# A hybrid decoder block on one core: mixer A's scores as three products of split operands, with selected and local keys side by side

## What is computed

```python
p_cmp = softmax(q_raw @ kc)                      # compressed keys, 15 of them
o_cmp = p_cmp @ vc
ks = rope(k_slc)                                 # selected branch: 256 tokens are 4 blocks,
p = softmax(mask(q_rot @ ks)); o_slc = p @ vs    # top 16 of 4 blocks, so all causal keys
num, _, den = band_attention(q_rot, rope(k_win), v_win, 511)   # local branch: window over 256 tokens
o = gates[..., 0:1] * o_cmp + gates[..., 1:2] * o_slc + gates[..., 2:3] * num / den
```

## Time and profile before

| what | value |
|---|---|
| median of 3 executions | 1837.71 us |
| the profiled execution | 1837.62 us, span 1835.8 us |
| granted TensorE clock | full (1.00) over the span |
| TensorE busy | 1824.1 us, 99% |
| VectorE, ScalarE, GpSimd busy | 1062.3, 823.3, 188.8 us |
| DMA | 344.78 MB, 188 GB/s on average |

### The profile page before, as it was taken

One profiled execution on the slowest core, in us unless ns is written; L12 is line 12 of the kernel. 1 busy time (PEld: TensorE's weight loads), 2 busy tenths in 40 slices (PEclk: granted clock), 3 DMA queues, 4 the chain that ended last, 5 costly groups with the idle time before them and its releaser, 6 DMA issues.

```text
span 1835.8 us, 23379 instructions
## 1 busy us (share of the span) xinstructions
PE 1824.1 (99%) x8474; PEld 1512.7 (82%) x8474; DVE 1062.3 (58%) x1097; ACT 823.3 (45%) x1062; POOL 188.8 (10%) x161
## 2 busy tenths in 40 slices
PE   9999999999999999999999999999999999999998
PEld 7888878888888888888888888888888888888886
DVE  7856656556665665644564456445644584445444
ACT  6644454444544435444444444444444464444442
POOL 2220002200202020022002200220022000000000
PEclk9999999999999999999999999999999999999999
DMA  9866677546455464666566656665666667776665
GB/s 290 249 194 186 190 230 222 167 124 189 129 168 164 128 182 127 183 186 193 162 193 186 193 162 192 187 191 163 188 190 190 177 184 218 211 210 204 214 206 193
DMA packets 183928, 344.78 MB, mean 188 GB/s; under 512 B 15136, under 2 KB 19360, under 8 KB 183840
## 3 DMA queue, kind: packets, MB, share of 16 engines
q1 hardware_dynamic: 182992, 342.45, 64.1%
q10 hardware_dynamic: 848, 1.07, 0.2%
HBM read 339.27 MB, written 4.19 MB: 187 GB/s over the span
## 4 chain that ended last, share of the span: by engine, by line
PE 98%; DVE 1%; DMA 0%; ACT 0%; issue 0%; DVEq 0%; ACTq 0%
PE acc L445 30%; PE acc L447 30%; PE acc L446 30%; PE trans L459 2%; PE heads L488 2%; PE scores L473 2%; PE acc L606 1%; PE heads L527 0%; DVE y L1291 0%; PE scores L595 0%; PE scores L506 0%; DMA xt_raw<-in_x_t 0%; PE trans L516 0%; ACT w_parts L717 0%; PE trans L649 0%
## 5 line engine op out<-in xcount | busy, mean ns | idle before, releaser
L947 DVE TENSOR_TENSOR w_parts<-raw,w_parts 128x1024 fp32r<-128x1024 f32 x624 | 779.9, 1251 | 695.6 <-ACT w_parts L717 695.2
L717 ACT ACTIVATE w_parts<-raw 128x1024 fp32r<-128x1024 f32 x624 | 660.3, 1059 | 735.3 <-PE acc L447 728.3
L445 PE MATMUL acc<-w_parts,x_parts 128*128 128x512 f32 x2432 | 961.1, 395 | 3.7 <-DVE w_parts L947 1.7
L447 PE MATMUL acc<-w_parts,x_parts 128*128 128x512 f32 x2432 | 948.2, 390 | 0.0
L446 PE MATMUL acc<-w_parts,x_parts 128*128 128x512 f32 x2432 | 947.0, 389 | 0.0
L447 PEld LDWEIGHTS acc<-w_parts,x_parts 128*128 128x128 f32 x2432 | 456.5, 188 | 97.4
L445 PEld LDWEIGHTS acc<-w_parts,x_parts 128*128 128x128 f32 x2432 | 456.9, 188 | 96.2 <-issue 5.0
L446 PEld LDWEIGHTS acc<-w_parts,x_parts 128*128 128x128 f32 x2432 | 457.1, 188 | 91.3
L400 POOL TENSOR_TENSOR rot<-tok_a,trig 128x512 f32<-128x512 f32 x26 | 41.1, 1579 | 1127.6 <-ACT tok_a L723 936.3
L729 ACT ACTIVATE probs_t<-trans 128x512 f32<-128x512 f32 (+1 forms) x44 | 26.2, 596 | 88.0 <-PE trans L459 81.0
L1199 DVE RECIPROCAL mixed<-mixed 128x256 f32<-128x256 f32 x32 | 55.9, 1747 | 0.5
(11 more groups left out here) (151 smaller groups left out, 581.2 us busy)
## 6 DMA issues: line engine op xcount, KB each, us to landing
raw<-in_w_in SPq DMA_DIRECT2D x480, 512.0 KB, 3.6
raw<-in_w_out SPq DMA_DIRECT2D x128, 512.0 KB, 4.5
raw<-in_w SPq DMA_DIRECT2D x16, 512.0 KB, 4.5
x_tok<-in_x SPq DMA_DIRECT2D x16, 256.0 KB, 4.9
xt_raw<-in_x_t SPq DMA_DIRECT2D x7, 512.0 KB, 5.9
out<-y SPq DMA_DIRECT2D x5, 512.0 KB, 2.9
wpost<-in_post_w SPq DMA_DIRECT2D x8, 256.0 KB, 4.9
gate_raw<-in_w_in SPq DMA_DIRECT2D x1, 768.0 KB, 8.0
```

What stands on the lines that cost most here:

```text
L445: nc.tensor.matmul(o, stat_hi, w_hi[:, s, kk, 0:width], start=(k == 0), stop=False)
L447: last = nc.tensor.matmul(o, stat_lo, w_hi[:, s, kk, 0:width], start=False, stop=(k == KB - 1))
L717: nc.scalar.activation(w_hi[:, n % SPLIT_SLOTS, :, 0:width], raw[:, n % RAW_SLOTS, :, 0:width], ACT.Copy).then_inc(hi_ready, 1)
L947: V.tensor_tensor(w_lo[:, s, :, 0:width], raw[:, n % RAW_SLOTS, :, 0:width], w_hi[:, s, :, 0:width].bitcast(F32), ALU.subtract).then_inc(l ...
```

## The change

Queries and keys of mixer A's selected and local branches are kept as first parts and rests (`q_hi`, `q_lo`, `k_hi`, `k_lo`), and the keys of both branches lie side by side, so that one product takes a head's query against both branches. A unit is now one tile and both branches: 2 heads of tile 0 (2 x 2 x 128 keys) or 1 head of tile 1 (2 x 256 keys); there are again six. Where a unit was 2 or 4 float32 matmuls it is 3 or 6 of F32R operands. The first parts come from ScalarE (`first_parts`, in the place of the old copies), the rests from VectorE (`rest_parts`), behind its split of the step; `tr_free` is counted up by VectorE for these fills. The selected keys are copied as they are and split later in two big operations. The values' products keep their number. Mixer B only has its arguments renamed.

```diff
+PAIRED = [(0, 0, 2), (0, 2, 2), (1, 0, 1), (1, 1, 1), (1, 2, 1), (1, 3, 1)]
...
+        k_hi, _ = sb("k_hi", [P, 2, HPG, SEQ], F32R, offset=late)
+        k_lo, _ = sb("k_lo", [P, 2, HPG, SEQ], F32R, offset=region + 4 * KB // 2 * SEQ)
+        q_hi, _ = sb("q_hi", [P, HPG, SEQ], F32R, offset=r_off)
+        q_lo, _ = sb("q_lo", [P, HPG, SEQ], F32R, offset=region + 4 * KB // 2 * SEQ + 4 * 2 * HPG * SEQ)
+        ksl_t, _ = sb("ksl_t", [P, HPG, SEQ], offset=p_off)
...
+            def paired_scores(u, unit, g, fills):
+
+                t, h0, nh = PAIRED[u]
+                pe.wait_ge(tr_free, fills)
+                pe.wait_ge(scores_free, unit)
+                nk = P * (t + 1)
+                for i in range(nh):
+                    o = scores[:, 2 * nk * i:2 * nk * (i + 1)]
+                    q = [part[:, h0 + i, t * P:(t + 1) * P] for part in (q_hi, q_lo)]
+                    keys = [part[:, :, g, 0:nk] for part in (k_hi, k_lo)]
+                    nc.tensor.matmul(o, q[0], keys[0], start=True, stop=False)
+                    nc.tensor.matmul(o, q[0], keys[1], start=False, stop=False)
+                    last = nc.tensor.matmul(o, q[1], keys[0], start=False, stop=True)
+                last.then_inc(scores_done, 1)
+
+            def paired_values(u, g, fill):
+
+                t, h0, nh = PAIRED[u]
+                pe.wait_ge(tr_free, fill + 1)
+                for i in range(nh):
+                    for branch in range(2):
+                        for b in range(t + 1):
+                            blk = (2 * i + branch) * (t + 1) + b
+                            last = nc.tensor.matmul(heads[:, t, (h0 + i) * P:(h0 + i + 1) * P],
+                                                    probs_t[:, u % 2, blk * P:(blk + 1) * P],
+                                                    v_tok[:, branch, b, bass.ds(P * g, P)],
+                                                    start=False, stop=(branch == 1 and b == t), skip_group_check=True)
+                return last
...
                 if 6 <= n <= 11:
                     u = n - 6
-                    keys = lambda h, nk: k_t[:, u // 3, g, 0:nk]
-                    unit_scores(u % 3, unit + 1 + u, qrot_t, keys, fill + 4)
+                    if u == 0:
+                        pe.wait_ge(ksplit_ready, 1)
+                    paired_scores(u, unit + 1 + u, g, fill + 4)
...
+            def first_parts(fill, dst, ready):
+
+                act.wait_ge(tr_done, fill + 1)
+                nc.scalar.activation(dst, trans[:, :].rearrange("p (h t) -> p h t", h=HPG), ACT.Copy).then_inc(ready, 1)
...
-                    take_fill(FILL_KSL + t, k_t[:, 0, :, t * P:(t + 1) * P])
+                    take_fill(FILL_KSL + t, ksl_t[:, :, t * P:(t + 1) * P])
...
+                if at == 1:
+                    act.wait_ge(weights_used, PAIRS * (C_CMP + 1))
+                    nc.scalar.activation(k_hi[:, 0, :, :], ksl_t[:, :, :], ACT.Copy).then_inc(khi_ready, 1)
...
-                    take_fill(FILL_KW[t], k_t[:, 1, :, t * P:(t + 1) * P])
+                    first_parts(FILL_KW[t], k_hi[:, 1, :, t * P:(t + 1) * P], khi_ready)
...
                     if at in (4, 5):
-                        take_fill(fill + at - 2, qrot_t[:, :, (at - 4) * P:(at - 3) * P])
+                        first_parts(fill + at - 2, q_hi[:, :, (at - 4) * P:(at - 3) * P], qhi_ready)
...
+            def rest_parts(fill, dst, hi, ready, count):
+
+                dve.wait_ge(tr_done, fill + 1)
+                dve.wait_ge(ready, count)
+                V.tensor_tensor(dst, trans[:, :].rearrange("p (h t) -> p h t", h=HPG), hi.bitcast(F32), ALU.subtract
                                 ).then_inc(tr_free, 1)
...
+                if at == 1:
+                    dve.wait_ge(khi_ready, 1)
+                    V.tensor_tensor(k_lo[:, 0, :, :], ksl_t[:, :, :], k_hi[:, 0, :, :].bitcast(F32), ALU.subtract
+                                    ).then_inc(ksplit_ready, 1)
+                if at in (5, 8):
+                    t = (at - 5) // 3
+                    cols = slice(t * P, (t + 1) * P)
+                    rest_parts(FILL_KW[t], k_lo[:, 1, :, cols], k_hi[:, 1, :, cols], khi_ready, 2 + t)
...
                     split(c, n)
+                    if at in (4, 5):
+                        cols = slice((at - 4) * P, (at - 3) * P)
+                        rest_parts(fill + at - 2, q_lo[:, :, cols], q_hi[:, :, cols], qhi_ready, TILES * g + at - 3)
```

More of the change, by code:

```diff
@@ L222, in build @@
         tr_free = sem("tr_free")
+        qhi_ready = sem("qhi_ready")
+        khi_ready = sem("khi_ready")
+        ksplit_ready = sem("ksplit_ready")
         scores_done = sem("scores_done")
@@ L531, in attention_a @@
                     u = n - 10
-                    values = lambda h, b: v_tok[:, u // 3, b, bass.ds(P * g, P)]
-                    last = unit_values(u % 3, u, values, fill + 6 + u, False, u >= 3)
+                    last = paired_values(u, g, fill + 6 + u)
                     if n == PAIRS - 1:
@@ L729, in take_fill, with exp_unit @@
                 nc.scalar.activation(dst, src, ACT.Copy, scale=scale).then_inc(tr_free, 1)
-            def exp_unit(u, slot, unit):
-                t, h0, nh = UNITS[u]
+            def first_parts(fill, dst, ready):
+                act.wait_ge(tr_done, fill + 1)
+                nc.scalar.activation(dst, trans[:, :].rearrange("p (h t) -> p h t", h=HPG), ACT.Copy).then_inc(ready, 1)
+            def exp_unit(t, slot, unit):
                 nk = P * (t + 1)
+                nh = NC // nk
                 act.wait_ge(max_ready, unit + 1)
@@ L839, in attention_a_frame @@
                     if 6 <= at <= 11:
-                        exp_unit((at - 6) % 3, (at - 6) % 4, unit + 1 + at - 6)
+                        exp_unit(PAIRED[at - 6][0], (at - 6) % 4, unit + 1 + at - 6)
             def mixing_frame(c, tiles_mixed):
@@ L872, in _ @@
                         u = (at - 1) // 2
-                        exp_unit(u, u, UNIT_B + u + UNITS_B * g)
+                        exp_unit(UNITS[u][0], u, UNIT_B + u + UNITS_B * g)
             def square(n, parity):
@@ L1117, in _, with mask_unit @@
             evacuate(C_QA0, 0, tok_a[:, 1, :], rq1)
-            def mask_unit(u, slot, unit, bias):
-                t, h0, nh = UNITS[u]
+            def mask_unit(t, slot, unit, bias):
                 nk = P * (t + 1)
+                nh = NC // nk
                 b = (bias[:, 0:P] if t == 0 else bias[:, P:3 * P]).unsqueeze(1).broadcast_to([P, nh, nk])
@@ L1129, in mask_unit, with normalise_unit @@
                 V.tensor_reduce(negmax[:, slot, 0:nh], p, AX.X, ALU.max, negate=True).then_inc(max_ready, 1)
-            def normalise_unit(u, slot, unit, recips, weights=None, gate=None):
-                t, h0, nh = UNITS[u]
+            def normalise_unit(t, slot, unit, recips, weights=None, gate=None):
                 nk = P * (t + 1)
+                nh = NC // nk
                 p = probs[:, slot, :].rearrange("p (h n) -> p h n", h=nh)
@@ L1140, in normalise_unit @@
                 if gate is not None:
-                    V.tensor_tensor(weight[:, slot, 0:nh], f, gate, ALU.mult).then_inc(weight_done, 1)
+                    w = weight[:, slot, 0:nh]
+                    V.tensor_tensor(w.rearrange("p (h b) -> p h b", b=2), f.rearrange("p (h b) -> p h b", b=2), gate,
+                                    ALU.mult).then_inc(weight_done, 1)
                     f = weight[:, slot, 0:nh]
@@ L1144, in normalise_unit, with attention_a_frame @@
                 V.tensor_tensor(p, p, f.unsqueeze(2).broadcast_to([P, nh, nk]), ALU.mult).then_inc(probs_ready, 1)
-            def attention_a_frame(c, g, unit):
+            def attention_a_frame(c, g, unit, fill):
                 for n in range(LEAD, PAIRS + LEAD):
@@ L1165, in attention_a_frame @@
                         u = at - 6
-                        mask_unit(u % 3, u % 4, unit + 1 + u, causal)
+                        mask_unit(PAIRED[u][0], u % 4, unit + 1 + u, causal)
                     split(c, n)
+                    if at in (4, 5):
+                        cols = slice((at - 4) * P, (at - 3) * P)
+                        rest_parts(fill + at - 2, q_lo[:, :, cols], q_hi[:, :, cols], qhi_ready, TILES * g + at - 3)
                     if at == 4:
@@ L1181, in attention_a_frame @@
                         u = at - 7
-                        t, h0, nh = UNITS[u % 3]
-                        normalise_unit(u % 3, u % 4, unit + 1 + u, 6 * g + u, 6 * g + u,
-                                       gates[:, t, bass.ds(HPG * g + h0, nh), 1 + u // 3])
+                        t, h0, nh = PAIRED[u]
+                        normalise_unit(t, u % 4, unit + 1 + u, 6 * g + u, 6 * g + u,
+                                       gates[:, t, bass.ds(HPG * g + h0, nh), 1:3])
             def mix_tile(at, group):
@@ L1233, in _ @@
                         u = (at - 1) // 2
-                        mask_unit(u, u, UNIT_B + u + UNITS_B * g, dilated)
```

(1 more changed line is left out.)

9 lines of the change are left out of this document (5 added, 4 removed).

## The result

The changed kernel takes 1842.38 us (median of 11 runs, 1842.01 to 1843.09) against 1838.1 us for the kernel before (11 runs, 1837.61 to 1840.09): a ratio of 1.0024, with a 95% interval from 1.0016 to 1.0031. It is slower by 4.3 us.

A forecast was written before the change was run, and what follows sets the result against it. The prediction took TensorE, busy 99%, to bound the kernel. Waits of 7.9, 0.9 and 0.4 us less 4.1 for cheaper scores gave +5.1 on 1837.62, so 1842.7 us, with an 8-in-10 range of 1838.4 to 1846.0.

The forecast's parts named there:

- TensorE is the bound: Whole kernel: TensorE is busy 99% of the span, so a wait put into its queue is paid in full.
- The eight waits: Mixer A, steps 5 and 6 of four frames: TensorE waits 0.98 and 1.00 us for banks VectorE frees; 7.9 us.
- The turn of 4.19: Mixer A, step 4 to 5: time in us from transposes through VectorE's rest to TensorE's next transposes, against 3.21 before.
- All six terms: Mixer A's bank chain: to copy 0.63, ScalarE split 0.49, VectorE split 1.09, next operation 1.14, rest 0.69, hand-over 0.15 us.
- The third case: Rival, mixer A's bank chain: shorter than added up, about 0.5 us a wait, 1838.4 us; chance 0.13.
- The gain: Mixer A's scores: units fall from 0.855 us to 0.69 (tile 0) and 0.68 (tile 1); 4.1 us over four frames.
- The case in which 256 columns cost as much as 512: Rival, tile 0's score products: no cheaper at half the width, 5.4 us more, 1848.1 us; chance 0.08.
- The keys' wait at step 9 of C_QA0: Local keys in C_QA0: the rest ends at 327.24, TensorE goes on at 327.39 instead of 326.48; 0.9 us.
- The selected keys' rest: C_QA0, step 1: VectorE's 1024-column rest delays the split and copy of `hidden`, so TensorE waits 0.4 us; bounds 0 to 0.9.
- The rule of the Trainium skill: VectorE's next operation starts only once the pipe is empty: each of nine turns 0.09 us longer, +5.9 instead of +5.1.
- The issue gap of the Trainium skill: Score products on TensorE: 0.109 us for 256 columns and 0.216 for 512, which would make the saving 4.9 us.
- Faster, if the waits do not bind: Rival, mixer A's bank: the rest runs ahead of VectorE's split, only cheaper scores remain, 1833.5 us; chance 0.06.

The follow-up runs named there:

- the hand-over: Kernel before, float32 scores kept, but a VectorE subtraction behind its split frees the rotated queries' bank at steps 4 and 5 of mixer A's frames: 1845.74 us.
- the second subtraction: Changed kernel with one more unused VectorE subtraction ahead of each rest of the rotated queries, eight in all: 1846.94 us.
- the product left out: Changed kernel with rests ahead of VectorE's splits, without the product of queries' first parts and keys' rests: 1828.11 us.
- one branch a product: Changed kernel with rests ahead of VectorE's splits, each score product over one branch's keys, twice as many at half the width: 1839.24 us.
- the selected keys' second subtraction: Changed kernel with one more unused 1024-column VectorE subtraction for the selected keys at step 1 of C_QA0: 1843.83 us.
- the version with the rests first: Changed kernel with VectorE's rests of rotated queries and local keys ahead of its split of the same step, all work kept: 1833.63 us.

## Why the prediction was right, and where not

The forecast was +5.1 us, by the waits; measured are +4.3 between the medians and +4.4 between the spans. Put right term by term, as below, its sum is 8.0 + 0.8 + 0 - 4.3 = +4.5. By its steps:

- **TensorE is the bound.** Right. Edits that put time between TensorE's instructions or took it away were paid nearly one to one: the hand-over 8.07 for 8.0, the second subtraction 4.56 for 4.8, the product left out 5.52 for 5.5. Two came out higher than expected, one branch a product with 5.6 for 5.0 and the selected keys' second subtraction with 1.45 for 0.94; what is known of the difference stands with them.
- **The eight waits, 7.9 us.** Measured 8.0 in steps (0.97 and 1.03 in the first frame) and 8.07 when put in alone. The turn of 4.19 was 4.18 and 4.22. All six terms held, the hand-over of 0.15 and the rest at 0.68 for 0.69 among them. The third case, waits of half the size, falls.
- **The gain, 4.1 us.** Measured 1.08 a frame, 4.3 us; the median of the version with the rests first is 4.0 under the kernel before. A product of 256 columns costs 0.117, taken at 0.115; the difference lies in steps 8 and 9, which were given the mean of the other four units and save 0.44 us together where the sum had 2 x 0.855 - 2 x 0.68 = 0.35. The case in which 256 columns cost as much as 512 falls.
- **The keys' wait at step 9 of C_QA0, 0.9.** It is 0.81 (4.10 against 3.29 us). The chain up to the rest was right; TensorE went on nearer to its end than 0.15 us:

```profile
322.94 0.60 PE L469 MATMUL trans<-cst,rot 128*128 128x128 f32 x4
326.30 0.68 DVE L1011 TENSOR_TENSOR k_lo<-trans,k_hi 128x512 fp32r<-128x512 f32 x1
327.04 1.92 PE L688 MATMUL trans<-w_sb,gelu 128*16 128x128 f32 x16 [0.74 <-DVE k_lo L1011]
```

  The rest ends at 326.98, and TensorE's next instruction starts 0.06 later.
- **The selected keys' rest, 0.4 us.** This is the mis-sized term: it costs nothing. The prediction let the split behind it run at 1.65 us, because the one of the kernel before did, beside GpSimd. In the changed kernel VectorE's queue has no gap there, and it is GpSimd that takes longer. Its subtraction for the rotation of the local keys, in the changed kernel, with VectorE's three operations beside it and TensorE's step 3:

```profile
301.72 5.62 POOL L414 TENSOR_TENSOR rot<-rot,rot_tmp 128x256 f32<-128x256 f32 x1
304.40 1.21 DVE L1163 TENSOR_TENSOR k_lo<-ksl_t,k_hi 128x1024 fp32r<-128x1024 f32 x1
305.53 1.21 DVE L994 TENSOR_TENSOR w_parts<-raw,w_parts 128x1024 fp32r<-128x1024 f32 x1
306.67 0.41 DVE L1147 COPY hidden<-trans 128x256 f32<-128x256 f32 x1
307.43 0.99 PE L667 MATMUL trans<-cst,junk 96*128 96x48 f32 x8
```

  The same operation of GpSimd, in the kernel before:

```profile
301.95 3.35 POOL L404 TENSOR_TENSOR rot<-rot,rot_tmp 128x256 f32<-128x256 f32 x1
```

  It is stretched from 3.35 to 5.62 us and ends 0.60 us after the recorded end of VectorE's last long subtraction, and rest and split both run at 1.21 us. This is the lower end that the prediction had named for this term, 0. The copy of `hidden` ends at 307.08, and TensorE's step 3 comes 3.66 us after step 2, as before. One more such subtraction was needed to see a wait.
- **The rule of the Trainium skill (VectorE: DVE Perf Modes, The DRAIN you can't avoid).** The forecast named an estimate of +5.9 for it. The section adds, as the forecast did not, that an operation which is not held starts earlier. Here too the rest starts 1.14 us after a split of 1.23, and the nine turns have no 0.09 more in them. The measurements stand against taking the rule into such a chain.
- **The issue gap of the Trainium skill (TensorE: Matmul & The Clock Gate, Back-to-back issue gap).** By it the estimate of the gain was 4.9; measured are 4.3. Its 0.109 at 256 columns is 0.117 here, its 0.216 at 512 is 0.227. The section gives these as gaps of an isolated matmul, and 0.131 us at 512 for a stream of weight loads and matmuls; the measured 0.227 is further from that.
- **Faster, if the waits do not bind.** The case had named what it takes, a rest ahead of the split, and 1833.5 us for it. The change does not do that; the kernel that does takes 1833.63.

## What to carry to other kernels

When a buffer with one slot changes the engine that frees it, add up the whole chain from the producer's start to its next turn: every operation that stands ahead of the new last one in its queue, and those ahead of what that one waits for, and compare with the producer's own step. A saving on the bound engine can be real (4.3 us here) and be outweighed twice over by such a turn that is 1 us too long; moving one operation ahead of its neighbour, on either engine, got it back here. In this kernel split operands paid in tile 0 only because the products stayed wide: price the product at its real width before replacing a float32 one.

## What the runs showed of the hardware

- A product of the split type costs 0.227 us at 512 columns, 0.117 at 256 and 0.111 at 128. Halving the width from 256 to 128 brings next to nothing: three products of 128 columns (0.33 us) are dearer than the two instructions of one float32 matmul (2 x 0.11).
- GpSimd's subtraction beside step 2 of C_QA0 starts inside a stretch in which VectorE runs operations without a gap. It takes 3.35 us in the kernel before, 5.62 with two subtractions of 1024 columns more in that stretch and 6.74 with three more, and ends 0.60, 0.60 and 0.59 us after the recorded end of the stretch's last long subtraction, while VectorE's take 1.21 each. The row with three more:

```profile
302.25 6.74 POOL L415 TENSOR_TENSOR rot<-rot,rot_tmp 128x256 f32<-128x256 f32 x1
```

  It is not always GpSimd that takes longer. In the kernel before, the splits that started behind a gap at 305.35 and 309.01, with GpSimd at work, took 1.73 and 1.68, and in the changed kernel the split at 360.00, directly behind another operation of VectorE, took 1.76 beside GpSimd's operation of 359.85. What decides between the two was not tried.
- The list of waits shows less than a wait costs: 6.6 us for eight that cost 8.0, since the modelled end of the last matmul covers about 0.17 us of each.
